# A two-layer trunk kernel: later norms summed token by token, scale and shift on ScalarE

## What is computed

```python
def rms_norm(x, g):
    xf = x.astype(F32)
    y = xf * lax.rsqrt(jnp.mean(xf * xf, axis=-1, keepdims=True) + EPS)
    return (y * g.astype(F32)).astype(x.dtype)
...
        zx = modulate(rms_norm(x, norm1_g[l]), mx[0], mx[1])      # z * (1 + scale) + shift
        zc = modulate(rms_norm(h, norm1_g[l]), mc[0], mc[1])
...
        x = x + mx[2] * (jnp.concatenate([ret_x, att_x, cm_x], axis=-1) @ w_out[l])
        x = x + mx[5] * swiglu(modulate(rms_norm(x, norm2_g[l]), mx[3], mx[4]), w_gate[l], w_up[l], w_down[l])
...
    return rms_norm(x, final_norm_g)
```

## Time and profile before

| | |
|---|---|
| median of 3 runs | 1971.47 us (1967.23 to 1972.42) |
| the profiled execution | 1968.78 us |
| its span, first to last instruction | 1967.0 us |
| busy: matmuls / DVE / ScalarE / GpSimd | 87% / 39% / 27% / 28% of the span |
| mean granted clock of TensorE | 0.931 of 2.4 GHz |

### The profile page before, as it was taken

One profiled execution on the slowest core, in us unless ns is written; L12 is line 12 of the kernel. 1 busy time (PEld: TensorE's weight loads), 2 busy tenths in 40 slices (PEclk: granted clock), 3 DMA queues, 4 the chain that ended last, 5 costly groups with the idle time before them and its releaser, 6 DMA issues.

```text
span 1967.0 us, 22403 instructions
## 1 busy us (share of the span) xinstructions
PE 1710.1 (87%) x9042; PEld 1361.6 (69%) x9042; DVE 758.0 (39%) x1220; ACT 524.7 (27%) x837; POOL 559.8 (28%) x252
## 2 busy tenths in 40 slices
PE   4789985777969999999999987995779689999997
PEld 2567764444857888888888876775556577878785
DVE  3441153554372222222222365525553723332425
ACT  3212123454223111111111122333443332222222
POOL 0612133000244233223322213235001553443431
PEclk8789997899989999999999996897799889999998
DMA  6534530000053222233333110221000312313121
GB/s 236 174 109 142 155 108 1 1 1 1 22 171 105 88 85 72 101 107 107 107 107 107 43 43 22 64 64 43 0 1 22 107 65 76 116 64 128 64 86 43
DMA packets 122190, 155.17 MB, mean 79 GB/s; under 512 B 20352, under 2 KB 89872, under 8 KB 122128
## 3 DMA queue, kind: packets, MB, share of 16 engines
q1 hardware_dynamic: 122128, 154.32, 24.3%
HBM read 152.21 MB, written 2.10 MB: 78 GB/s over the span
## 4 chain that ended last, share of the span: by engine, by line
PE 74%; DVE 12%; ACT 7%; issue 2%; SPq 2%; POOL 1%; DMA 1%; DVEq 0%; ACTq 0%; POOLq 0%
PE ps L1389 15%; PE ps L1390 15%; PE ps L1391 15%; PE ps L1650 5%; PE ps L1651 5%; PE ps L1652 5%; PE ps L1600 2%; ACT s_at L746 2%; PE ps L1329 2%; ACT pT L519 1%; DVE hl L1268 1%; PE ps L1574 1%; DVE s_at L1197 1%; PE ps L1671 1%; PE ps L1672 1%
## 5 line engine op out<-in xcount | busy, mean ns | idle before, releaser
L413 POOL TENSOR_TENSOR wl<-raw,wh 128x1024 fp32r<-128x1024 f32 x144 | 353.9, 2471 | 1041.2 <-ACT wh L519 1041.2
L1389 PE MATMUL ps<-zh,wh 128*128 128x512 f32 x1632 | 592.7, 363 | 37.8 <-DVE zl L979 16.7
L1390 PE MATMUL ps<-zl,wh 128*128 128x512 f32 x1632 | 587.3, 360 | 0.0
L1391 PE MATMUL ps<-zh,wl 128*128 128x512 f32 x1632 | 583.5, 358 | 0.0
L1389 PEld LDWEIGHTS ps<-zh,wh 128*128 128x128 f32 x1632 | 314.6, 193 | 122.2 <-issue 49.4
L1391 PEld LDWEIGHTS ps<-zh,wl 128*128 128x128 f32 x1632 | 314.0, 192 | 46.4
L1390 PEld LDWEIGHTS ps<-zl,wh 128*128 128x128 f32 x1632 | 315.0, 193 | 43.4
L519 ACT ACTIVATE wh<-raw 128x1024 fp32r<-128x1024 f32 x144 | 148.7, 1058 | 399.9 <-PE ps L1391 290.7
L1281 DVE SCALAR_TENSOR_TENSOR xT<-ps,modcol,xT 128x512 f32<-128x512 f32 (+1 forms) x264 | 169.2, 661 | 104.1 <-PE ps L1652 100.4
L1262 DVE TENSOR_TENSOR hf<-gs,ps 128x512 f32<-128x512 f32 x66 | 37.6, 597 | 403.4 <-ACT gs L790 403.3
L1650 PE MATMUL ps<-hh,wh_d 128*128 128x512 f32 x480 | 173.4, 361 | 11.4 <-DVE xT L1281 11.4
(11 more groups left out here) (220 smaller groups left out, 1777.8 us busy)
## 6 DMA issues: line engine op xcount, KB each, us to landing
raw<-in_w_gate_dram SPq DMA_DIRECT2D x22, 1024.0 KB, 7.0
raw<-in_w_up_dram SPq DMA_DIRECT2D x22, 1024.0 KB, 9.4
raw_m<-in_w_mod_dram SPq DMA_DIRECT2D x22, 1024.0 KB, 5.2
raw_d<-in_w_down_dram SPq DMA_DIRECT2D x20, 1024.0 KB, 5.0
raw<-in_w_in_dram SPq DMA_DIRECT2D x14, 1024.0 KB, 5.4
raw<-in_w_mod_dram SPq DMA_DIRECT2D x11, 1024.0 KB, 5.3
raw_n<-in_w_mod_dram SPq DMA_DIRECT2D x9, 1024.0 KB, 5.2
raw<-in_w_out_dram SPq DMA_DIRECT2D x32, 256.0 KB, 4.4
```

What stands on the lines that cost most here:

```text
L413: nc.gpsimd.tensor_tensor(dst, src, hi.bitcast(F32), ALU.subtract).then_inc(sem(done), 1)
L1389: MM(dst, wt_h[:, h, w], zh[:, k, c0:c1], start=(k == 0), stop=False)
L1390: MM(dst, wt_h[:, h, w], zl[:, k, c0:c1], start=False, stop=False)
L1391: last = MM(dst, wt_l[:, h, w], zh[:, k, c0:c1], start=False, stop=(k == KC - 1))
```

## The change

Norm 0 stays as it is, in functions of its own (`first_norm`, `first_norm_hi`). In norms 1 to 4:

- DVE makes seven adds. TensorE multiplies each 128-token tile of `nacc`, as weights, by two columns of ones, and then adds the same with the eighth square from `nsq`: sums with tokens on partitions, two columns per tile, in bank 5.
- ScalarE's root and DVE's reciprocal work on `rstd`, 128 partitions by 12 columns (8 in norms 3 and 4).
- TensorE spreads them back: one column of `rstd`, broadcast to 128 columns as weights, times the identity, one product per 128 tokens, into banks 6 and 7.
- Per tile, DVE multiplies xT by these rows in PSUM into `nxr` (two buffers), ScalarE applies scale and shift twice with the function Identity, into `zh` (rounded) and into `nxz`, each in the pieces of 512 and 256 columns, and DVE subtracts for `zl`, for all eight k. GpSimd has no part in it.
- `ffn_mod(0, 0)` moves behind the first FFN step.

The core of the diff, in the order ScalarE, DVE, TensorE:

```diff
+        def squares_before(u):
+
+            return KC * u - max(u - 1, 0)
...
             def norm_root(u, W):
                 act.wait_ge(sem("nst_mm"), u + 1)
+                if u:
+                    tiles = W // P
+                    nc.scalar.activation(rstd[:, 0:2 * tiles], ps[:, 5, 0:2 * tiles], ACT.Sqrt, bias=epsc[:, 0:1], scale=1.0 / D
+                                         ).then_inc(sem("nrms_rdy"), 1)
+                    return
...
-            def norm_hi(u, W):
-                nxz = (norm_later if u else norm_start)[3]
-                for k in range(KC):
-                    act.wait_ge(sem("nzf_rdy"), 8 * u + k + 1)
-                    copy(zh[:, k, 0:W], nxz[:, k % 3, 0:W]).then_inc(sem("zh_rdy"), 1)
+            def norm_z(u, W):
+                nxr, nxz = norm_later[2:4]
+                sh = 48 * (u // 2) + KC * (3 if u % 2 else 0)
+                for k in range(KC):
+                    act.wait_ge(sem("nzf_rdy"), 8 * u + k + 1)
+                    if k >= 3:
+                        z_wait(act, u, k - 3)
+                    for dst in (zh[:, k, :], nxz[:, k % 3, :]):
+                        for c0, c1, s in [(0, SX, 0)] + ([(SX, NT, 1)] if W == NT else []):
+                            last = nc.scalar.activation(dst[:, c0:c1], nxr[:, k % 2, c0:c1], ACT.Identity,
+                                                        bias=modcol[:, sh + k, s:s + 1], scale=acol[:, k, s:s + 1])
+                    last.then_inc(sem("zh_rdy"), 1)
...
+            def norm(u, W):
+
+                nxr, nxz = norm_later[2:4]
+                if u < 4:
+                    modulated_gain(u)
+                norm_recip(u, W)
+                rows = ps[:, 6:8, :].rearrange("p b n -> p (b n)")[:, 0:W]
+                dve.wait_ge(sem("rstd_mm"), u)
...
+                for k in range(KC):
+                    if k >= 2:
+                        dve.wait_ge(sem("zh_rdy"), 8 * u + k - 1)
+                    V.tensor_tensor(nxr[:, k % 2, 0:W], xT[:, k, 0:W], rows, ALU.mult).then_inc(sem("nzf_rdy"), 1)
+                    if k:
+                        lo(k - 1)
+                lo(KC - 1)
...
             def norm(u, W):
...
+                tiles = W // P
+                pe.wait_ge(sem("nacc_rdy"), squares_before(u) + KC - 1)
+                for t in range(tiles):
+                    MM(ps[:, 5, 2 * t:2 * t + 2], nacc[:, P * t:P * t + P], ones[:, 0:2], start=(t == 0), stop=False,
+                       skip_group_check=True)
+                pe.wait_ge(sem("nsq_rdy"), 8 * u + KC)
+                for t in range(tiles):
+                    last = MM(ps[:, 5, 2 * t:2 * t + 2], nsq[:, (KC - 1) % 2, P * t:P * t + P], ones[:, 0:2], start=False,
+                              stop=True, skip_group_check=True)
+                last.then_inc(sem("nst_mm"), 1)
+                pe.wait_ge(sem("nrms_inv"), u + 1)
+                for t in range(tiles):
+                    dst = ps[:, 6, P * t:P * t + P] if t < 4 else ps[:, 7, P * (t - 4):P * (t - 4) + P]
+                    last = MM(dst, rstd[:, 2 * t:2 * t + 1].to_broadcast([P, P]), eye, start=True, stop=True)
+                last.then_inc(sem("rstd_mm"), 1)
...
                 def ffn_first():
                     a, b = A_GATE[l], B_UP[l]
-                    if l == 0:
-                        ffn_mod(0, 0)
...
                     if l == 0:
+                        ffn_mod(0, 0)
                         ffn_mod(0, 1)
```

More of the change, by code:

```diff
@@ L151, in trunk @@
         xr_start = xin[:, :, :].rearrange("p t d -> p (t d)").rearrange("p (k n) -> p k n", k=KC)
-        norm_bufs = [("pad_a", [P, 2, NT], F32), ("nsq", [P, 2, NT], F32), ("nrb", [P, NT], F32), ("pad_b", [P, NT], F32),
+        norm_bufs = [("pad_a", [P, 2, NT], F32), ("nsq", [P, 2, NT], F32), ("nxr", [P, 2, NT], F32),
                      ("nacc", [P, NT], F32), ("nxz", [P, 3, NT], F32)]
         overlay(norm_bufs)
-        norm_later = tuple(made[n] for n in ("nsq", "nacc", "nrb", "nxz"))
+        norm_later = tuple(made[n] for n in ("nsq", "nacc", "nxr", "nxz"))
         Z_DVE = (0,)
@@ L450, in _ @@
             lo_a(0, 1)
-            norm(0, NT)
+            first_norm()
             with pool.Fori(1, NP_IN + 1) as a:
@@ L456, in _ @@
                 if l:
-                    norm(2, NT)
                     for a in range(A_IN[l] + 1, A_OUT[l] + 1):
@@ L493, in _ @@
                 lo_b(B_UP[l], 1)
-                norm(2 * l + 1, NT if l == 0 else SX)
                 def ffn_step(s, first=False, last=False):
@@ L602, in _ @@
                     hi_a(0, 1, "ld_in0", ld[1], first=True)
-                    norm_hi(0, NT)
+                    first_norm_hi()
                 else:
-                    norm_hi(2, NT)
+                    norm_z(2, NT)
                 a0 = A_IN[l]
@@ L874, in add_square @@
                 ins.then_inc(sem("nacc_rdy"), 1)
-            def norm_parts(W):
-                return [(0, SX, 0)] + ([(SX, NT, 1)] if W == NT else [])
             def norm_recip(u, W):
-                nrb = (norm_later if u else norm_start)[2]
                 dve.wait_ge(sem("nrms_rdy"), u + 1)
-                V.reciprocal(nrb[:, 0:W], nrb[:, 0:W]).then_inc(sem("nrms_inv"), 1)
-                dve.wait_ge(sem("nrms_inv"), u + 1)
+                root = rstd[:, 0:2 * (W // P)] if u else norm_start[2][:, 0:W]
+                V.reciprocal(root, root).then_inc(sem("nrms_inv"), 1)
             def log_decay_a():
@@ L1002, in _ @@
                 W = NT if l == 0 else SX
-                norm(2 * l, NT)
+                if l:
+                    norm(2, NT)
+                else:
+                    first_norm()
                 nt = W // P
@@ L1340, in norm @@
             def norm(u, W):
-                nacc = (norm_later if u else norm_start)[1]
-                pe.wait_ge(sem("nacc_rdy"), 8 * u + 8)
-                for c0, c1, s in ([(0, SX, 0)] + ([(SX, NT, 1)] if W == NT else [])):
-                    last = MM(ps[:, s, 0:c1 - c0], ones, nacc[:, c0:c1], start=True, stop=True)
-                last.then_inc(sem("nst_mm"), 1)
+                nsq, nacc = (norm_later if u else norm_start)[0:2]
+                if u == 0:
+                    pe.wait_ge(sem("nacc_rdy"), 8)
+                    for c0, c1, s in [(0, SX, 0), (SX, NT, 1)]:
+                        last = MM(ps[:, s, 0:c1 - c0], ones, nacc[:, c0:c1], start=True, stop=True)
+                    last.then_inc(sem("nst_mm"), 1)
+                    return
+                tiles = W // P
[7 more added lines that the diff above has]
+                              stop=True, skip_group_check=True)
+                last.then_inc(sem("nst_mm"), 1)
+                pe.wait_ge(sem("nrms_inv"), u + 1)
[3 more added lines that the diff above has]
+                last.then_inc(sem("rstd_mm"), 1)
             pe.wait_ge(sem("ld_x"), 48)
```

91 lines of the change are left out of this document (47 added, 44 removed).

## The result

| | before | changed |
|---|---|---|
| median (4 runs each) | 1970.03 us (1967.23 to 1972.42) | 1950.36 us (1948.04 to 1953.43) |
| ratio | | 0.9902, 95% interval 0.9881 to 0.9922 |
| profiled execution, its span | 1968.78, 1967.0 us | 1951.23, 1949.4 us |
| mean granted clock | 0.931 | 0.939 |

A forecast was written before the change was run, and what follows sets the result against it. TensorE, 87% busy, bounds the kernel through its waits in norms 1 to 4 (A to D). 2.1 + 11.0 + 1.7 + 1.15 + 1.0 = 17.0 us off 1968.78 gives 1951.8; forecast 1953 us, range 1944 to 1962.

The forecast's parts named there:

- Term 6: Norm 2's z tiles: interval falls from 3.18 to 1.95 us; seven intervals win 8.6 us.
- handover: Rival, 16%: ScalarE's pieces do not overlap or each tile passes both engines in full; interval 2.8 us, total 1959.
- Term 2: Token-major sums on TensorE: 5.6 us in norm 1, 5.2 in norm 2, 3.7 in norm 3, 3.4 in norm 4.
- clock holds: Rival, 12%: small products keep TensorE's clock up in norms 2 and 4, sums and spreads at double speed; 6.6 more, 1946.
- weights one after another: Rival, 4%: each small product's two weight loads stand in line, near 0.95 us a product; 12 slower, 1982.
- Terms 3 and 4: Norms 1 to 4: root and reciprocal together 0.6 us; spreading back 2.8, or 1.9 in norms 3 and 4.
- Term 5: First z tile through multiplication, ScalarE's pieces and remainder: 4.0 us with handovers, in norm 3 2.9.
- Term 7: Norm 2: TensorE's clock may be up before the eighth tile; 1.0 us taken of a possible 2.1.
- Term 8: Norm 3: first multiplication, reading one operand from PSUM, no longer stands behind GpSimd; otherwise norm 3 loses its 1.7 us.
- Term 9: Modulation product behind the first FFN step adds about 1.06 us within a 2.90 us wait; costed at nothing.
- Term 1: Norms 1 to 4: the eighth add (0.95 us in norm 2) goes; TensorE's sums start at the seventh add's end.
- handed back: Rival, 5%: TensorE reaches its next wait earlier and stands there; only 3 to 5 of 17 us remain, 1966.

The follow-up runs named there:

- Experiment 5: Changed kernel with norm 2's ScalarE pieces in different forms by tile (scale and shift, copy, neither, scale alone, shift alone); 1950.92 us in one execution.
- 9: Changed kernel with the scale moved from ScalarE to DVE's multiplication, ScalarE's pieces adding only the shift; 1949.61 us, ratio 0.9907 to the kernel before.
- experiment 12: Changed kernel without the new buffer rstd, root and reciprocal going into columns of nacc; 1947.92 us, ratio 0.9883 to the kernel before.
- experiment 2: Changed kernel's z path alone, with wide sums, root and reciprocal as before and multiplication from an SBUF row; 1961.82 us, ratio 0.9949 to the kernel before.
- experiment 4: Changed kernel with the eighth square added on DVE again and one group of TensorE sums; 1948.55 us, ratio 0.9887 to the kernel before.
- experiment 3: Changed kernel with fills, unread products in TensorE's waits in norms 1 to 4; 1939.46 us, ratio 0.9833 to the kernel before.
- experiment 11: Changed kernel with eight adds, unread products, scale on DVE, and a 256-column unread product behind every second two-column product; 1941.05 us, ratio 0.9860.
- experiment 1: Changed kernel's token-major sums alone, with scale and shift on DVE and remainders on GpSimd as before; 1957.18 us, ratio 0.9919 to the kernel before.
- experiment 6: Changed kernel with nxz of tiles 2 and 5 made by DVE instead of ScalarE in norms 1 to 3; 1951.60 us, ratio 0.9888.

## Why the prediction came out

**Right in sum, by errors that cancel.** 17.0 us were foreseen, 16.7 found in the stages. That the profiled execution too came within 0.6 us of the forecast's 1951.8 is luck: without the 3.6 us of scatter ahead of A the two profiles would lie 14.0 us apart. Of the signs that I had named, one failed, the distance of B's tiles (2.4 us, where I had asked for 1.9 to 2.1), and the first product on them came 13.2 us after layer 0's last product, where I had asked for 12 to 13.

- *Term 6, the interval, was mis-sized,* and it is the largest. "ScalarE has 1.7 to 1.8" took the price of plain copies for operations with a scale and a shift. It is 2.40, so B's interval is 2.38 instead of 1.95, and 5.6 us came instead of 8.6. Experiment 5 has the cause, 9 the test. The case found lies halfway to the rival "handover", though not by its mechanism: ScalarE never stood idle. The Trainium skill, "VectorE: DVE Perf Modes", section on the TRN2 errata, whose fixed cost per ScalarE operation I had worked out to 2.03 us for four pieces, was nearer than my rows; the trace has 2.40, and for copies 1.68. It was nearer by chance: it was taken without the overlap of 0.1 a piece, and with it the estimate falls to some 1.7, the copies' price.
- *Term 2, the sums, was too dear,* by 1.7 us in B (3.5 against 5.2) and 1.4 in D (2.0 against 3.4). The price of 0.47 at half clock was right (A 5.3 against 5.6), but I let the clock fall one or two products after TensorE resumed. In B it held for nine (in experiment 12 for all twelve), in D for all eight. The rival "clock holds" had the direction, for half a stage. The rival "weights one after another" is out: 0.23 a product at full clock, 0.43 at half.
- *Terms 3 and 4:* 0.7 and 2.9 (C 2.1), as forecast within 0.2. The reciprocal takes 0.23 where it took 4.96.
- *Term 5, the first tile:* 4.6 instead of 4.0, and in C 3.9 instead of 2.9, by ScalarE's pieces again and, in C, by a remainder of 1.49 beside GpSimd.
- *Term 7:* 1.4 instead of 1.0, and by the way foreseen: the clock was up before the eighth tile and fell again. The size is chance: in experiment 12, with the same code there, this stretch takes 3.70 us, where the changed kernel has 2.63.
- *Term 8 held.* C's first multiplications take 0.64 each beside GpSimd's remainder, where one took 2.73, and experiment 2 gets the stall back with an SBUF row. This agrees with the Trainium skill, "SBUF — State Buffer", section on who interferes with whom.
- *Term 9 held:* from the start of `ffn_mod`'s product to `mod_finish` it is 3.98 us against 3.96 before (610.48 to 614.44). The products there grew from one half of 1.06 to two of 1.92 together and the wait shrank from 2.90 to 2.05:

```profile
605.02 1.92 PE L1370 MATMUL ps<-raw_m,cz 128*32 128x512 f32 x16
...
609.00 1.02 PE L1378 MATMUL ps<-sel,modrow 128*128 128x2 f32 x8 [2.05 <-DVE modrow L872]
```

- *Term 1, the saved eighth add,* read as no cost at all, is paid for by six products that cost more than the add wherever the clock is down (experiment 4).

- *Left out:* the allocation of `rstd`, which I read as free, costs 1.6 us in layer 0's FFN (experiment 12). The 3.6 us ahead of A are scatter, as the stages say.

The rival "handed back", TensorE waiting anew, did not come about as a wait: A's gain is there at `mod_finish` (52.75 from R, 54.6 before), and behind B's eighth tile the clock is up sooner. But by the clock's turns A's gain can shrink on the way: in experiment 5, with the changed kernel's code up to there, it is 54.15.

**Best version.** The change with fills (experiment 3), 1939.46 us, beats both kernels: its interval ends at 0.9865, below the 0.9881 at which the change's begins. Eight adds and the scale on DVE shorten its stages further, and `rstd` in another place takes back 1.6 us; the medians here cannot show so little, and the three were not run together.

## What to carry to other kernels

Take the price of an operation from a row of the same form: on ScalarE a per-partition scale or shift cost 0.09 us each beyond a copy, which on four pieces a tile moved the bound from one engine to another. Make statistics small before root and reciprocal (0.23 us for 12 columns against 4.96 for 768), even where TensorE needs more products for it. When a serial stretch has been cut, look at TensorE's clock in it: unread products in its waits gave another 10 to 11 us, more than half of what the whole change gave.

## What the runs showed of the hardware

- A two-column fp32 product costs TensorE 0.23 us at granted clock 1.00 and 0.43 at 0.50, from one start to the next, nearly all of it outside its two columns: the spread's products of 128 columns follow each other at 0.22 (experiment 11, B) and 0.43 (the changed kernel).
- Behind 24 such records without a gap, preceded by a wait of 1.23 us, the clock fell from 1.00 to 0.50 for three microseconds (experiment 3); behind one and the same wait of 2.05 us it fell in nine traces (the changed kernel's among them) and not in four (experiments 1, 2, 5 and 6), which is worth 1.6 us. Executions of one code can differ by that much in this place alone.
- 48 bytes a partition, allocated ahead of the operands of `down`, made its records 1 to 2 ns longer on average, 1% (in the three passes of 512 columns 6 ns longer, 3 shorter and 4 longer).
- DVE's scale and shift on SBUF operands takes 0.87 us for 512 and 256 columns with GpSimd at rest (experiment 6) and 2.37 beside GpSimd's remainder (experiment 1). The trace of before has both, 0.87 at 1183.32 ahead of GpSimd's first remainder and 2.36 at 1190.89; I used only the second, so leaving it on DVE looked dearer than it is once GpSimd is out.
- DVE's two-multiplier operation with a PSUM row costs 1.13 us for 512 and 256 columns, against 0.95 for one multiplication of 768.
